# Two attentions of a transformer program, from one head at a time to pairs of heads: reciprocals after the values, gate rows through memory, mask in the bias

## What is computed

```
# neighbourhood attention (NA): head size 64, a learned bias, and a window of 16 columns on a 64-wide grid
s = q @ k.T * 64**-0.5 + bias[head];  s = where(in_window, s, -1e30)
y = softmax(s) @ v                     # per head, 256 x 256 scores
x = x + gate[2] * (y @ w_o)            # gate: one row of 1024 for all tokens

# latent attention (MLA): 64 + 32 columns of q and k per head, values of 64
s = q @ k.T * 96**-0.5;   y = softmax(s) @ v;   x = x + gate[2] * (y @ w_o)
```

## Time and profile before

| | us |
|---|---|
| median of 3 runs | 1607.41 (1606.31 to 1607.64) |
| the profiled execution, its own time | 1608.82 |
| its span in the profile | 1606.9 |
| TensorE busy | 1553.6 (97%) |
| VectorE, ScalarE, GpSimd busy | 1167.8, 866.2, 116.6 |
| NA, first scores to first product of `project` | 677.33 to 733.40 |
| MLA, the same | 999.16 to 1046.99 |

### The profile page before, as it was taken

How to read it: one execution, slowest core, us unless ns; L and a number is a source line. 1 busy time by engine, 2 the same in 40 slices (tenths; PEclk the granted TensorE clock), 3 DMA queues, 4 the chain that set the end, 5 groups by cost and what they waited for, 6 DMA issues and landing times.

```text
span 1606.9 us, 24289 instructions
## 1 busy us (share of the span) xinstructions
PE 1553.6 (97%) x10100; PEld 1339.7 (83%) x10100; DVE 1167.8 (73%) x1364; ACT 866.2 (54%) x1009; POOL 116.6 (7%) x138
## 2 busy tenths in 40 slices
PE   7999999989999999998999999999999999999998
PEld 7999989877999989856999986578888888888886
DVE  5767769755667676455776653668888988997997
ACT  6343466442543354344434442457777677777775
POOL 0100013210000000061000001700000000000000
PEclk9999999989999999999999999999999999999999
DMA  8877733212688764504777750039998998998993
GB/s 343 316 291 273 255 114 132 73 56 82 278 331 300 298 235 163 178 1 174 300 269 295 271 188 1 1 106 371 340 368 311 368 359 306 370 337 322 370 342 140
DMA packets 52063, 386.80 MB, mean 241 GB/s; under 512 B 5904, under 2 KB 6240, under 8 KB 8048
## 3 DMA queue, kind: packets, MB, share of 16 engines
q1 hardware_dynamic: 50544, 376.68, 63.1%
q0 software_dynamic: 1408, 8.54, 1.4%
HBM read 384.15 MB, written 1.05 MB: 240 GB/s over the span
## 4 chain that ended last, share of the span: by engine, by line
PE 90%; DVE 5%; ACT 3%; issue 1%; DMA 1%; POOL 1%; DVEq 0%; ACTq 0%
PE bank L302 25%; PE bank L304 24%; PE bank L303 24%; PE bank L1285 4%; PE bank L1860 2%; PE bank L1819 1%; PE bank L1850 1%; PE bank L2022 1%; PE bank L1982 1%; PE bank L2329 1%; PE bank L543 1%; PE bank L2363 1%; DVE sb_wlo L269 1%; ACT sb_whi L265 1%; PE bank L2032 0%
## 5 line engine op out<-in xcount | busy, mean ns | idle before, releaser
L269 DVE TENSOR_TENSOR sb_wlo<-sb_raw,sb_whi 128x2048 fp32r<-128x2048 f32 x137 | 313.8, 2292 | 181.6 <-ACT sb_whi L265 181.4
L302 PE MATMUL bank<-sb_xhi,sb_whi 128*128 128x256 f32 x1344 | 382.7, 285 | 4.0 <-DVE sb_xlo L585 2.0
L303 PE MATMUL bank<-sb_xlo,sb_whi 128*128 128x256 f32 x1344 | 380.6, 283 | 0.0
L304 PE MATMUL bank<-sb_xhi,sb_wlo 128*128 128x256 f32 x1344 | 380.5, 283 | 0.0
L265 ACT ACTIVATE sb_whi<-sb_raw 128x2048 fp32r<-128x2048 f32 x137 | 261.4, 1909 | 160.2 <-PE bank L304 156.4
L302 PEld LDWEIGHTS bank<-sb_xhi,sb_whi 128*128 128x128 f32 x1344 | 258.1, 192 | 8.4 <-issue 4.6
L303 PEld LDWEIGHTS bank<-sb_xlo,sb_whi 128*128 128x128 f32 x1344 | 258.3, 192 | 1.2
L304 PEld LDWEIGHTS bank<-sb_xhi,sb_wlo 128*128 128x128 f32 x1344 | 258.2, 192 | 0.0
L2293 DVE TENSOR_TENSOR sb_wlo<-sb_raw,sb_whi 128x2048 fp32r<-128x2048 f32 x84 | 190.8, 2284 | 12.6 <-ACT sb_whi L2287 12.0
L302 PE MATMUL bank<-sb_whi,sb_slots_hi 128*128 128x512 f32 x448 | 181.3, 405 | 0.0
L304 PE MATMUL bank<-sb_whi,sb_slots_lo 128*128 128x512 f32 x448 | 175.9, 393 | 0.0
(11 more groups left out here) (460 smaller groups left out, 2439.2 us busy)
## 6 DMA issues: line engine op xcount, KB each, us to landing
sb_raw<-in_ffn SPq DMA_DIRECT2D x98, 1024.0 KB, 5.4
sb_raw<-in_moe SPq DMA_DIRECT2D x86, 1024.0 KB, 6.5
sb_ada_raw<-in_ada SPq DMA_DIRECT2D x32, 1536.0 KB, 8.6
sb_cst<-in_moe SPq DMA_DIRECT2D x28, 1024.0 KB, 6.6
sb_xn<-in_moe SPq DMA_DIRECT2D x27, 1024.0 KB, 6.8
sb_ada_raw<-in_moe SPq DMA_DIRECT2D x27, 1024.0 KB, 7.0
sb_raw<-in_w_in SPq DMA_DIRECT2D x13, 1024.0 KB, 4.8
sb_raw<-in_na_qk SPq DMA_DIRECT2D x8, 1024.0 KB, 4.9
```

The costliest lines, as they stand in the source:

```text
L269: e.tensor_tensor(wlo[s][:, :], raw[s][:, :], whi[s][:, :], ALU.subtract).then_inc(s_lo[s], 1)
L302: e.matmul(dst, wh, xh, start=first, stop=False, skip_group_check=skip)
L303: e.matmul(dst, wh, xl, start=False, stop=False, skip_group_check=skip)
L304: return e.matmul(dst, wl, xh, start=False, stop=last, skip_group_check=skip)
```

## The change

It rewrites `attend`, moves the mask, and makes the gate rows in another way.

- **Pairs of heads.** A round handles two heads. The queues get the order `score(n)`, the maxima of both, the exponentials of the first head; then the inverse of the sums of pair n-1; `weigh` and `scaled` of pair n-2; the transposes and `inverse_rows` of pair n-1, and the copies out of PSUM, one head by ScalarE and one by VectorE; the exponentials of the second head; `spread_rows` of pair n-1; and after every second pair `split_pair`. Instructions of the two heads alternate in `score` (NA only), `inverse_rows` and `weigh`.
- **Reciprocals after the values.** The exponentials are transposed as they are. TensorE spreads the inverted sums over the output partitions by a product with the identity (`inverse_rows`, two matmuls for each head, in banks 6 and 7), ScalarE copies them out, and VectorE multiplies them into the product with the values (`scaled`), in place of the copy at L1867. GpSimd has nothing left to do in `attend`.
- **Scale.** The negated maximum comes from the reducing instruction itself; the factor of MLA is in its table "turned".
- **Mask.** GpSimd adds the window to the bias, 16 additions of 128 x 512 elements behind the four pieces of the bias (each with a semaphore of its own now), in the feed-forward layer ahead of NA. L1817 is gone.
- **Gate rows.** SP writes two columns of `mod` to memory as rows, element by element, waits for that, and reads each row back to all 128 partitions. These stand in SP's queue between `linear` (or `latent`'s part) and the loads of `project`, and wait for the engines to have finished the part ahead of `attend`.
- **Table.** An exponential on one column (`exp_table`) ahead of `linear` and of the queries loads ScalarE's table early.

The diff, with the old `attend` left out (it is shown above):

```diff
...
+    attn = {"window": np.where((k >= first) & (k < first + WIN_W), 0.0, NEG)}
...
+    attn |= {"turned": both * np.float32(QH) ** -0.5, "cos": cos, "sin": sin, "place": place, "placeturn": placeturn}
...
+        def exp_table():
+
+            act.step(lambda e: e.activation(first_exp[:, :], epss[:, 0:1], ACT.Exp))
...
+        gate_store = nc.dram_tensor("gate_store", (2, 2, KT, P), F32, kind="Internal").ap()
+        m_mod = {}
+
+        def gate_rows(layer, first_dst, second_dst, *free):
+
+            s_put, s_got = sem(f"gates_stored{layer}"), [sem(f"gate_row{layer}_{i}") for i in range(2)]
+            sp.wait(m_mod[layer], *free)
+
+            def run(e):
+
+                for i, part_ in enumerate((2, 5)):
+                    e.dma_start(gate_store[layer, i].rearrange("k p -> p k"), mod[:, layer, part_ * KT:(part_ + 1) * KT],
+                                allow_slow_non_contiguous=True).then_inc(s_put, 16)
+                e.wait_ge(s_put, 32)
+                for i, dst in enumerate((first_dst, second_dst)):
+                    row = gate_store[layer, i]
+                    e.dma_start(dst, bass.AP(tensor=row.tensor, offset=row.offset, ap=[[0, P], [1, D]])).then_inc(s_got[i], 16)
+
+            sp.plain(run)
+            return [(s, 16) for s in s_got]
...
+    def score(n):
+        turns = [(i, q) for q in range(NB) for i in both(n)] if bias is not None else [(i, q) for i in both(n) for q in range(NB)]
+        for i, q in turns:
+            m_score[i] = pe.step(lambda e, i=i, q=q: e.matmul(part(i, q), *scores(i, q), start=True, stop=True),
+                                 *m_ready(i), m_sread.get(i - 2))
...
+            m_max[i] = dve.step(lambda e: e.reduce_max(mx[:, i, 0:2], src, AX_X, negate=True), m_score[i])
...
+    def inverse(n):
+        at = 2 * n
+        m_rec[n] = dve.step(lambda e: e.reciprocal(mx[:, at:at + 2, 2:4], mx[:, at:at + 2, 2:4]), m_exp[at], m_exp[at + 1])
...
+    def inverse_rows(n):
         for q in range(NB):
...
+            for i in both(n):
+                m_bc[n] = pe.step(lambda e, q=q, i=i: e.matmul(
+                    bank[6 + n % 2][i % 2 * HD:(i % 2 + 1) * HD, q * P:(q + 1) * P],
+                    mx[:, i, 2 + q:3 + q].broadcast_to([P, HD]), ident, start=True, stop=True), m_rec[n], m_spread.get(n - 2))
+
+    def kept(i):
+        src = bank[2 + i % 2][:, :].rearrange("p (k q) -> p k q", k=NB)
+        if i % 2 == 0:
+            m_pt[i] = act.step(lambda e: e.activation(pt[0], src, ACT.Copy), m_tr[i], m_pv.get(i // 2 - 1))
+        else:
+            m_pt[i] = dve.step(lambda e: e.tensor_copy(pt[1], src), m_tr[i], m_pv.get(i // 2 - 1))
+
+    def spread_rows(n):
+        m_spread[n] = act.step(lambda e: e.activation(spread[n % 2], bank[6 + n % 2][:, 0:T], ACT.Copy), m_bc[n], m_out.get(n - 2))
+
+    def weigh(n):
         for kb in range(NB):
...
+            for i in both(n):
+                m_pv[n] = pe.step(lambda e, kb=kb, i=i: e.matmul(
+                    bank[4 + n % 2][i % 2 * HD:(i % 2 + 1) * HD, 0:T], values(i, kb), pt[i % 2][:, kb, :],
+                    start=kb == 0, stop=kb == NB - 1), m_pt[i], m_out.get(n - 2))
+
+    def scaled(n):
...
+        m_out[n] = dve.step(lambda e: e.tensor_tensor(dst, b, a, ALU.mult), m_spread[n], m_pv[n])
 
     parts = []
...
+    for n in range(pairs + 2):
+        now, last, before = n < pairs, 1 <= n <= pairs, n >= 2
+        if now:
+            score(n)
+            largest(2 * n)
+            largest(2 * n + 1)
+            exponential(2 * n)
+        if last:
+            inverse(n - 1)
+        if before:
+            weigh(n - 2)
+            scaled(n - 2)
+        if last:
+            transposed(n - 1)
+            inverse_rows(n - 1)
+            kept(2 * n - 2)
+            kept(2 * n - 1)
+        if now:
+            exponential(2 * n + 1)
+        if last:
+            spread_rows(n - 1)
+        if before and n % 2:
+            at = n - 3
+            parts += env["split_pair"](at, m_out[at], m_out[at + 1])
+    return parts
...
+                m_b[q4, z] = pool.step(lambda e, part=part: e.tensor_tensor(
+                    part, part, win[:, :].rearrange("p (h t) -> p h t", h=1).broadcast_to([P, 2, T]), ALU.add),
+                    got_win, (got_bias[q4], 16))
...
+        m_row, m_row2 = env["gate_rows"](0, spare[:, 0:D], spare[:, D:2 * D], *env["scratch_free"][0])
...
+        m_row, m_row2 = env["gate_rows"](1, spare[:, 0:D], spare[:, 2 * D:3 * D], m_ks[AH // 2 - 1], m_qs[AH // 2 - 1], m_v)
```

More of the change, by code:

```diff
@@ L1118, in take_mod @@
             dve.wait(mt)
+            m_mod[layer] = mt
         def M(layer, i):
@@ new lines, in attend, with largest, exponential @@
+def attend(env, ctx, tag, scores, values, bias, m_ready, order=None):
+    sb, bank, pe, act, dve = (env[n] for n in ("sb", "bank", "pe", "act", "dve"))
+    ident, y, late = env["ident"], env["xn"], env["late"]
+    pairs = AH // 2
+    blocks = lambda at: late[:, at:at + NB * T].rearrange("p (b t) -> p b t", b=NB)
+    s = [env["h"][:, :, :], env["sil"][:, :, :], blocks(0), blocks(NB * T)]
+    pt = [env["rstd"][:, :, :], blocks(2 * NB * T)]
+    spread = [late[:, 3 * NB * T + i * T:3 * NB * T + (i + 1) * T] for i in range(2)]
+    mx = sb(f"mx_{tag}", [P, AH, 4], ctx=ctx)
+    m_score, m_max, m_exp, m_sread, m_tr, m_pt, m_rec, m_bc, m_spread, m_pv, m_out = ({} for _ in range(11))
+    both = lambda n: (2 * n, 2 * n + 1)
+    part = lambda i, q: bank[i % 2][:, q * T:(q + 1) * T]
+    def score(n):
[3 more added lines that the diff above has]
+                                 *m_ready(i), m_sread.get(i - 2))
+    def largest(i):
+        if bias is None:
+            src = bank[i % 2][:, :].rearrange("p (q t) -> p q t", q=NB)
+            m_max[i] = dve.step(lambda e: e.reduce_max(mx[:, i, 0:2], src, AX_X, negate=True), m_score[i])
+            return
+        for q in range(NB):
+            m_max[i] = m_sread[i] = dve.step(lambda e, q=q: e.tensor_tensor_reduce(
+                s[i % 4][:, q, :], part(i, q), bias[:, q, i, :], -1.0, 3e38, ALU.add, ALU.min,
+                mx[:, i, q:q + 1]), m_score[i], m_tr.get(i - 4))
+    def exponential(i):
@@ L1857, in weigh @@
-    def weigh(i):
-        hp, bk = i % 2 * HD, bank[4 + i // 2 % 2]
-        for kb in range(NB):
-            m = pe.step(lambda e, kb=kb: e.matmul(bk[hp:hp + HD, 0:T], values(i, kb), pt[i % 2][:, kb, :],
-                                                  start=kb == 0, stop=kb == NB - 1), m_tread[i], m_out.get(i // 2 - 2))
-        m_pv[i] = m
-        if i % 2:
-            dst, src = y[:, i // 2, :], bk[:, 0:T]
-            if order is not None:
-                dst, src = order(dst), src.rearrange("p (r c) -> p r c", c=GRID)
-            m_out[i // 2] = act.step(lambda e: e.activation(dst, src, ACT.Copy), m)
@@ L1869, in split @@
-    def split(n):
-        return env["split_pair"](2 * n, *[m_out[2 * n + z] for z in range(2)])
-    parts = []
-    for i in range(AH + 3):
-        if i < AH:
-            softmax(i)
-        if 0 <= i - 1 < AH:
-            normalised(i - 1)
-        if i < AH and i >= 3:
-            weigh(i - 3)
-        if 0 <= i - 2 < AH:
-            transposed(i - 2)
-        if i >= AH:
-            weigh(i - 3)
-        if i >= 7 and i % 4 == 3:
-            parts += split(i // 4 - 1)
-        follow(i)
@@ L1887, in attend, with transposed @@
-    return parts + split(AH // 4 - 1)
+    def inverse(n):
+        at = 2 * n
+        m_rec[n] = dve.step(lambda e: e.reciprocal(mx[:, at:at + 2, 2:4], mx[:, at:at + 2, 2:4]), m_exp[at], m_exp[at + 1])
+    def transposed(n):
+        for i in both(n):
+            bk = bank[2 + i % 2]
+            for kb in range(NB):
+                for q in range(NB):
+                    m = pe.step(lambda e, kb=kb, q=q, bk=bk, i=i: e.transpose(
+                        bk[:, kb * T + q * P:kb * T + (q + 1) * P], s[i % 4][:, q, kb * P:(kb + 1) * P], ident),
+                        m_exp[i], m_pt.get(i - 2))
+            m_tr[i] = m
@@ new lines, in spread_rows @@
+    def spread_rows(n):
+        m_spread[n] = act.step(lambda e: e.activation(spread[n % 2], bank[6 + n % 2][:, 0:T], ACT.Copy), m_bc[n], m_out.get(n - 2))
+    def weigh(n):
+        for kb in range(NB):
+            for i in both(n):
+                m_pv[n] = pe.step(lambda e, kb=kb, i=i: e.matmul(
+                    bank[4 + n % 2][i % 2 * HD:(i % 2 + 1) * HD, 0:T], values(i, kb), pt[i % 2][:, kb, :],
+                    start=kb == 0, stop=kb == NB - 1), m_pt[i], m_out.get(n - 2))
+    def scaled(n):
+        dst, a, b = y[:, n, :], spread[n % 2], bank[4 + n % 2][:, 0:T]
+        if order is not None:
+            dst, a, b = order(dst), *(z.rearrange("p (r c) -> p r c", c=GRID) for z in (a, b))
+        m_out[n] = dve.step(lambda e: e.tensor_tensor(dst, b, a, ALU.mult), m_spread[n], m_pv[n])
@@ L1902, in neighbourhood @@
         bias = sb("na_bias", [P, NB, AH, ROWS, GRID], ctx=ctx)
[L1903 to L1905 removed]
```

(2 more changed lines are left out.)

105 lines of the change are left out of this document (22 added, 83 removed).

## The result

The changed kernel takes **1582.37 us** (median of 4 runs, 1580.32 to 1584.43) against 1606.86 for the kernel before on the same chip: ratio 0.985, 95% interval 0.9833 to 0.9867. That is 24.5 us less where 31 were forecast. The direction and the range held; the point was 6 us too low. The profiled execution is the longest of the four, 1584.43 us, with a span of 1582.6.

What follows compares the result with a forecast made beforehand. TensorE, busy 97% of the span, was taken as the bound. 1608.82 less 21.9 (NA) and 9.6 (MLA) gave 1577.3 us for the profiled execution, which lies 1.4 above the median: 1576 us, range 1569 to 1588.

Steps and rivals of the forecast that it cites:

- TensorE's 3.61 us for a pair in NA: TensorE in NA: scores, values, transposes, reciprocals and four shape changes take 3.61 us a pair, against 5.56 before.
- Rival C: Both attentions: heads don't run side by side at 256 columns, TensorE's round is 5.78 us, time 1600; chance 0.06.
- MLA 4.48 us a round, 38.2 us in all: MLA: scores can't be paired, 4.48 us a pair against 4.92; stage 38.2 us against 47.83, 9.6 less.
- The long round through ScalarE, the split and the maxima: NA, every fourth head: VectorE's split half delays the next maxima; path 4.84 us, two rounds together 8.2 us.
- NA laid out, 34.2 us: NA with durations put in order of three queues: 34.2 us against 56.07, 21.9 us less.
- rival E: Small losses together: low clock in NA's first 7 us, GpSimd in VectorE's way, late stores: 1586; chance 0.06.
- The mask "costs nothing": Layer ahead of NA: 16 additions of 1.03 us on idle GpSimd, 16.5 us, add nothing to the time.
- Gate rows, cost 0: SP's queue: stores and reads delay weight loads to between 683 and 721, covered by the attentions, so nothing taken.
- Rival D: Gate-row stores take tens of us and hold the weights: slower from 31 us beyond the cover; chance 0.02.
- All other stages as long as before: Stages outside the two attentions: the change was to leave their lengths as they were.
- Rival B: Both attentions: clock falls to half for good, NA 55.0 us, MLA 67.5, time 1626, slower; chance 0.06.
- A: The forecast itself as likeliest case: 1569 to 1584 us; chance 0.80.

Runs made afterwards that it cites:

- a3: The changed kernel with the split's low halves on VectorE put behind the next pair's maxima: 1582.27 us, ratio 0.9839 to the kernel before.
- b5: The changed kernel with other TensorE work placed between the two heads' products: 1615.13 us, ratio 1.004 to the kernel before.
- a2: The changed kernel with a pair's heads one after the other in NA's scores, `weigh` and `inverse_rows`: ratio 0.9852 to the kernel before.
- a4: The changed kernel without the gate rows' transfers, nothing stored or read back: 1584.69 us, ratio 0.9861 to the kernel before.
- b4: The changed kernel with the early table load's one-number target kept inside the tile first_root: 1581.81 us, ratio 0.9835 to the kernel before.

## Why the prediction was right, and where it was off

- **TensorE's 3.61 us for a pair in NA: right.** A short round at full clock is 1.06 + 1.01 + 1.02 + 0.59 = 3.68 in the chain (689.40 to 693.09 in a3). Its ground, that two 256-column products run at the price of one, is shown by b5. I had taken the alternation in the program for the cause; a2 shows that the engine finds the pairs itself. Rival C is refuted.
- **MLA 4.48 us a round, 38.2 us in all: right** (4.54 and 37.97; the terms written down add to 38.1).
- **The long round through ScalarE, the split and the maxima: right**, in place and size: two rounds 8.16 us against 8.2.
- **NA laid out, 34.2 us: right for a full clock (33.86), wrong because the clock fell.** I counted the half-clock start among the things that go ("up to 3"), though nothing in the change keeps TensorE busy there. It came again, for 6.8 us or longer, in nine of the ten profiles of this change without filling products. Mis-sized term: 0 instead of 2.9 us. It had been put into rival E; the likeliest case should have had it. What else was to go from the start (table, gate rows, GpSimd's multiplications) is gone: the full-clock run pays for none of it.
- **The mask "costs nothing": wrong in price, nearly right in effect.** 2.04 us an addition in the mean, not 1.03, and 10.6 us more of VectorE's time (46.2 - 39.3 and 79.3 - 75.6), which cost TensorE 1.0. I let one row, L330 at 0.69 beside GpSimd in the earlier trace rows, outweigh the rule that VectorE and GpSimd hold each other up. That GpSimd instruction had one tile as input, the additions have two; whether this is the difference was not tried.
- **Gate rows, cost 0: right.** The stores landed after 10.2 us, within 2.1 to 16.8; the loads left at 688.2, within 683 to 721; without them nothing is won (a4). Rival D is refuted.
- **"All other stages as long as before": wrong by 2.5 us** in the experts, from a tile of one number that I had read as nothing. It was in the diff.
- **The sum.** 1577.3 against 1584.4 on the profiled execution, 7.1 us: attentions 2.3 (NA's clock 2.9, the rest -0.6), experts 2.5, mask 1.0, and 1.4 in stages that differ from one execution to the next or whose difference has no known cause (router 1.5, behind NA 1.6, first and third layer 1.6, mixer -2.6, linear products -0.7), with 0.1 of rounding. That the mixer's half clock was short in this execution, and so most of these cancel, is luck.

Rival B, the clock at half for good, is refuted: rounds with TensorE busy 25.65 of 27.20 us ran at full clock. The time lies inside A's range (1569 to 1584) and 3.6 us below E's 1586; the clock, the main part of E, is the largest single term that A's sum missed.

## What to carry to other kernels

Count what TensorE does for a unit of work, find the other engines' longest path beside it, and lay out the queues: that gave both attentions to 1 us where the clock was the same. Don't let a change's bonus include a half clock unless the change fills the idle time that comes ahead of it. Read each new tile, however small, as a shift of all tiles behind it, and compare stages that the change doesn't touch: the experts alone held 2.5 of the 7.1 us missed. To test whether two heads overlap, look at the starts of the instructions and not at their order in the program.

## What the runs showed that was not expected

- Products on different halves of the array overlap even when four instructions of one head stand in the queue ahead of the other's (a2, starts 0.01 us apart). The Trainium skill (TensorE: Matmul & The Clock Gate, Step-by-step: what each phase is for) says that matmuls stay in program order; across two halves these starts don't. Work of another shape between them does end the overlap (b5).
- With `slots_hi` and `slots_lo` 32 bytes further on, 896 products of 512 columns took 395 ns instead of 391 or 392, 1% (b4). The same move made the products with the odd `hlo` 2 ns shorter (392 for 394), so "off a multiple of 64 is slower" is no rule that these runs give.
- An addition of 512 columns on GpSimd and a sum on VectorE took turns, each waiting for the whole instruction of the other: 2.27 us for 1.30 and 2.30 for 1.22.
- The router took 23.8 to 28.2 us, the longer the more of it was at half clock (3.4 us in those up to 25.5, 13.7 in those from 28.0).
